# Gating and the front of a recurrent mixer moved into the input projection's stage

## Chip, cores and metric

The kernel runs on one core of a Trainium2 chip. The metric is device time in microseconds (us) of one execution, lower is better. TensorE is called PE here, VectorE DVE, ScalarE ACT, GpSimd Pool, SyncE SP.

## What is computed

A transformer block with a mixture of experts, then two layers (l = 0, 1) of a second block, on 256 tokens of width 1024 in f32. The part of a layer that the change touches:

```python
hn = rms_norm_2(h, g_mix[i])
z = hn @ w_in[i]                                   # 1024 x 2840
z_a, z_b, z_c = split_cols(z, (A_COLS, B_COLS, C_COLS))   # 512, 1024, 1304 columns
y_a = chunked_spatial_gating(z_a, ...)   # gelu, layer_norm of v, causal 128x128 mixing over tokens, times u
# rwkv7_time_mix(z_b, ...): its front
z = z_b + (z_prev - z_b) * mu                      # z_prev: the token before
r, k, v, wd, ad, gd = split_cols(z, B_SIZES)
w_logit = -softplus(-(w0 + tanh(wd) @ w_up)) - 0.5
decay = exp(-exp(w_logit)); a = sigmoid(a0 + ad @ a_up); g = sigmoid(gd) @ g_up
kk = k * k_k, normalised per head;  k = k * (1 + (a - 1) * k_a)
# then a recurrence over the tokens, done by chunks of 64 with cumulated decays
```

## The kernel before, in words

The program is a list of stages. Every engine walks through the list in its own order of instructions; at a stage's end (`end_stage`) all four wait for each other. Only SP, which streams weights from memory into a ring of nine buffers, runs ahead through all stages.

A projection (`stage_project`) takes 512 columns of the weight at a time (the last block of `w_in` is 280 wide), each block in two pieces of four row chunks (128x2048 elements; 128x1120 for the narrow block), so `in_l` has 12 pieces, numbered here 0 to 11. Products are taken in three passes of halves: ACT writes the upper part of a piece (`split_high`, L556), DVE the rest (`split_low`, L560), PE multiplies (L536 to L538), token tile 0 and then tile 1, 12 matmuls each. ACT takes each finished 128x512 result (a job, numbered q, two to a block) out of PSUM into `z` (L2188). In the loop of `evacuate`, iteration i splits the piece `group.size - 1` ahead of piece i, for which piece i - 1 must have been multiplied, and then takes out piece i's jobs where the block is complete. Before the change the group has four upper-part buffers, and the order of blocks is that of z_b and z_c first and z_a last.

After job 5 ACT issues five DMAs (`shift_act`, L2340 to L2344) which copy z_b down by one token into `w_prev`. Pool waits for them and mixes: three operations of 128x1024 for each of two token tiles (L2355 to L2359).

Behind the projection come three stages: `gating(l)`, `rwkv(l)` and `nsa(l)`. The gating has PE transposes (L2236), gelu on ACT (L2245, L2247), a layer norm on DVE, four small matmuls (L2240) and a multiplication on DVE. In `rwkv`, "the front" here is all up to the signal `rw_rkab` (L2614): low-rank inputs on ACT (L2526 to L2528), their transposes (L2369), six matmuls (L2374 to L2376), sigmoids (L2530), decays, cumulated decays by six matmuls and eight tiny ones (L2381, L2385), exponentials (L2538 to L2543), products on DVE (L2609 to L2614). PE's next step, sixteen transposes (L2391), waits for it.

## Time and profile before

| | us |
|---|---|
| median of 3 runs (lowest, highest) | 2702.75 (2701.73, 2703.71) |
| profiled execution, its time | 2700.91 |
| profiled execution, its span | 2699.1 |
| PE, DVE, ACT busy | 2377.1, 1828.3, 1458.9 |

The span runs from the first to the last instruction; the time of an execution holds 1.8 us more. An engine's busy time adds up its instructions over all stages, so it doesn't say which engine sets the pace in one of them.

### The profile page before, as it was taken

Reading aid. Unit: us, or ns where it says so; the run is one execution under the profiler, and the core shown is the slowest. Engines: PE = TensorE matmul, PEld = TensorE weight load, DVE = VectorE, ACT = ScalarE, POOL = GpSimd, SP = SyncE. Lnnn points to the kernel's source line nnn. Section 1 sums busy time; section 2 is a strip of 40 time slices with the busy share of each in tenths; the row PEclk is TensorE's granted clock in tenths of the full one; section 3 lists DMA queues with packets and bytes.
Section 4 is the critical chain, followed back from the end, with each engine's and each line's share of the span. In section 5 each row is a group of like instructions: output and inputs, shape, how many; then the busy total and the mean of one; then the engine's idle time right before and its main releaser. Section 6 shows DMA issues by size and latency. Waiting matters only on the chain. (4 is left out here: it accounts for less than half of the span.)

```text
span 2699.1 us, 30473 instructions
## 1 busy us (share of the span) xinstructions
PE 2377.1 (88%) x12398; PEld 1932.8 (72%) x12398; DVE 1828.3 (68%) x1848; ACT 1458.9 (54%) x1363; POOL 90.9 (3%) x57
## 2 busy tenths in 40 slices
PE   7688478699999999857899986787999999999996
PEld 6566366588888887646678775666888888888884
DVE  5444444688888887446555453557898888898884
ACT  4243122577777775423444443246677767767763
POOL 0200000000000000121000002100000000000000
PEclk9789688899999999868899998898999999999998
DMA  8035024399999998600555444024999998999990
GB/s 260 26 109 171 0 95 139 130 362 366 360 364 361 369 357 322 196 19 11 167 171 187 160 133 134 3 95 161 363 356 358 369 356 294 363 357 358 367 351 31
DMA packets 231968, 617.66 MB, mean 229 GB/s; under 512 B 23164, under 2 KB 68604, under 8 KB 194184
## 3 DMA queue, kind: packets, MB, share of 16 engines
q1 hardware_dynamic: 229728, 609.30, 64.2%
q10 hardware_dynamic: 2088, 6.28, 0.7%
q8 instruction: 102, 1.67, 0.2%
q14 instruction: 50, 0.41, 0.0%
HBM read 612.40 MB, written 1.05 MB: 227 GB/s over the span
## 5 line engine op out<-in xcount | busy, mean ns | idle before, releaser
L560 DVE TENSOR_TENSOR ring_parts<-ring,high_parts 128x2048 fp32r<-128x2048 f32 (+1 forms) x574 | 1287.2, 2284 | 232.4 <-ACT high_parts L556 212.8
L556 ACT CAST high_parts<-ring 128x2048 fp32r<-128x2048 f32 (+1 forms) x574 | 1078.7, 1897 | 258.6 <-PE ps L538 226.3
L538 PE MATMUL ps<-high_parts,arena_parts 128*128 128x512 f32 (+2 forms) x1560 | 618.7, 397 | 0.0
L536 PE MATMUL ps<-high_parts,hT_parts 128*128 128x512 f32 (+2 forms) x1120 | 448.8, 401 | 37.5 <-DVEq L440 22.1
L537 PE MATMUL ps<-ring_parts,hT_parts 128*128 128x512 f32 (+2 forms) x1120 | 443.3, 396 | 0.0
L536 PE MATMUL ps<-high_parts 128*128 128x512 f32 x912 | 365.3, 401 | 0.0
L537 PE MATMUL ps<-ring_parts,high_parts 128*128 128x512 f32 x912 | 359.1, 394 | 0.0
L538 PE MATMUL ps<-high_parts 128*128 128x512 f32 x912 | 356.5, 391 | 0.0
L538 PEld LDWEIGHTS ps<-high_parts,arena_parts 128*128 128x128 f32 x1560 | 298.1, 191 | 68.9
L536 PE MATMUL ps<-high_parts,arena_parts 128*128 128x512 f32 x744 | 294.7, 396 | 11.7 <-ACTq L440 4.5
L537 PE MATMUL ps<-ring_parts,arena_parts 128*128 128x512 f32 x744 | 293.3, 394 | 0.0
L536 PEld LDWEIGHTS ps<-high_parts,hT_parts 128*128 128x128 f32 x1120 | 215.8, 193 | 89.2 <-DVEq L440 25.0
L537 PEld LDWEIGHTS ps<-ring_parts,hT_parts 128*128 128x128 f32 x1120 | 215.7, 193 | 49.6 <-issue 0.2
L538 PEld LDWEIGHTS ps<-high_parts 128*128 128x128 f32 x912 | 171.4, 188 | 41.8
L536 PEld LDWEIGHTS ps<-high_parts 128*128 128x128 f32 x912 | 172.1, 189 | 37.7
L537 PEld LDWEIGHTS ps<-ring_parts,high_parts 128*128 128x128 f32 x912 | 171.0, 187 | 35.8
L536 PEld LDWEIGHTS ps<-high_parts,arena_parts 128*128 128x128 f32 x744 | 140.4, 189 | 45.9 <-ACTq L440 4.9
L537 PEld LDWEIGHTS ps<-ring_parts,arena_parts 128*128 128x128 f32 x744 | 140.6, 189 | 32.3
L2069 DVE SCALAR_TENSOR_TENSOR arena<-ps,arena 128x512 f32<-128x512 f32 x80 | 57.9, 723 | 147.7 <-PE ps L538 132.5
L1985 ACT CAST arena_parts<-ps 128x512 fp32r<-128x512 f32 x80 | 45.4, 567 | 140.3 <-PE ps L1883 140.3
L538 PE MATMUL ps<-high_parts,hT_parts 128*128 128x512 f32 x304 | 120.0, 395 | 0.0
L2003 ACT ACTIVATE arena<-ps 128x512 f32<-128x512 f32 x80 | 46.4, 580 | 68.2 <-PE ps L538 68.2
(523 smaller groups left out, 1932.6 us busy)
## 6 DMA issues: line engine op xcount, KB each, us to landing
ring<-in_moe_w SPq DMA_DIRECT2D x248, 1024.0 KB, 5.4
ring<-in_w_gate SPq DMA_DIRECT2D x64, 1024.0 KB, 5.9
ring<-in_w_up SPq DMA_DIRECT2D x64, 1024.0 KB, 5.7
ring<-in_w_down SPq DMA_DIRECT2D x64, 1024.0 KB, 5.8
ring<-in_w_in SPq DMA_DIRECT2D x46, 1024.0 KB, 5.1
ring<-in_ffn_w SPq DMA_DIRECT2D x44, 512.0 KB, 5.0
ring<-in_moe_w SPq DMA_DIRECT2D x32, 512.0 KB, 5.0
ring<-in_w_out SPq DMA_DIRECT2D x12, 1024.0 KB, 5.3
```

The source lines that it names most:

```text
L536: pe.matmul(dst, a_hi, b_hi, start=first, stop=False, skip_group_check=True)
L537: pe.matmul(dst, a_hi, b_lo, start=False, stop=False, skip_group_check=True)
L538: return pe.matmul(dst, a_lo, b_hi, start=False, stop=last, skip_group_check=True)
L556: act.copy(high_flat(p), raw_flat(p)).then_inc(upper, 1)
L560: dve.tensor_tensor(raw_flat(p, ring_parts_flat), raw_flat(p), f32(high_flat(p)), ALU.subtract).then_inc(split, 1)
L1985: act.copy(m_hidT[:, 0:st.n // P, :].rearrange("p c n -> p (c n)"), ps[:, TURN, 0:st.n])\
L2003: act.activation(m_sg[:, 0:st.n], ps[:, GATE, 0:st.n], ACT.Silu).then_inc(sig("moe_silu"), 1)
L2069: dve.scalar_tensor_tensor(out=m_hid[:, 0:st.n], in0=src, scalar=m_gate[:, q:q + 1], in1=m_sg[:, 0:st.n], op0=ALU.mult, op1=ALU.mult).then ...
```

## The change

`gating(l)` as a stage goes. Its operations and the whole front of `rwkv` become `front(l)`: hooks that the loops of the projection `in_l` call at written-out places. PE's hooks come after a token tile of a piece (slot = 2 x piece + tile): 6, 16, 17, 18 and 19. ACT's and DVE's hooks come in iteration i of `evacuate`, before the jobs are taken out (`after` = 0) or behind (`after` = 1). The blocks' order becomes z_b (pieces 0 to 3), z_a (4, 5), then z_c (6 to 11, the last two narrow). The upper-part buffers of `in_l` are three, not four. The shift DMAs are issued after job 3, not within job 5. Mixing of token tile 0 stays on Pool, tile 1 goes to DVE. Tanh is computed by a sigmoid; a mask `tri_aft` takes the place of `same_chunk`, so that one subtraction (L2607) and one copy (L2537) go. Results of the gating wait in `s_sq`, and Pool copies them to `ycat` at the start of `rwkv`.

```diff
-            blocks = [(c0, min(512, (width if c0 >= first else first) - c0))
-                      for c0 in list(range(first, width, 512)) + list(range(0, first, 512))]
+            starts = list(range(0, width, 512))
+            if first:
+                starts = starts[1:3] + starts[0:1] + starts[3:]
+            blocks = [(c0, min(512, width - c0)) for c0 in starts]
...
-            for groups in (group_in, group_out, group_ple):
-                groups.append(Group(4))
+            for groups, size in ((group_in, 3), (group_out, 4), (group_ple, 4)):
+                groups.append(Group(size))
...
+                    if hook:
+                        hook(pe, 2 * p.at + j.tile)
...
+                    hook(eng, i, 0)
+                for j in p.jobs if p.last else []:
...
-                        if after and j.q == after[0]:
-                            after[1](eng)
...
+                if hook:
+                    hook(eng, i, 1)
...
+                    dve.tensor_tensor(tri_aft[:], tri_aft[:], tri_inc[:], ALU.subtract)
...
-            group_in[l].high = highs(13872, 11824, 9776, 7728)
+            group_in[l].high = highs(13872, 11824, 9776)
...
+        MW.at = 15920
+        w_prev = MW.take(NT, 1024)
+        MW.at = 15920
+        w_R, w_K, w_A, w_Ke = [half_t() for _ in range(4)]
+        w_lw, w_a, w_g, w_kk, w_km, w_B, w_Be, w_lora = [half_t() for _ in range(8)]
...
+        def mix(eng, l, t):
+
+            done = sig("rw_mixing_pool" if t == 0 else "rw_mixing_dve")
+            zb_t = z[:, t, ZB0:ZC0]
+            eng.tensor_tensor(w_prev[:, t, :], w_prev[:, t, :], zb_t, ALU.subtract).then_inc(done, 1)
+            eng.wait_ge(done, 2 * l + 1)
+            eng.tensor_tensor(w_prev[:, t, :], w_prev[:, t, :], l_mu[:], ALU.mult).then_inc(done, 1)
+            eng.wait_ge(done, 2 * l + 2)
+            eng.tensor_tensor(zb_t, zb_t, w_prev[:, t, :], ALU.add).then_inc(sig("rw_mixed"), 1)
...
         def mix_pool(pool, l):
-
             pool.memset(w_prev[0:1, 0, :], 0.0).then_inc(sig("rw_first"), 1)
             pool.wait_ge(sig("rw_first"), l + 1)
-            pool.wait_ge(sig("rw_prev"), 80 * (l + 1))
...
-                pool.tensor_tensor(zb_t, zb_t, w_prev[:, t, :], ALU.add).then_inc(sig("rw_mixed"), 1)
+            mix_wait(pool, l)
+            mix(pool, l, 0)
...
+
+            def pe_(pe, slot):
+                if slot == 6:
+                    pe.wait_ge(sig("layer_params"), 16 * N_LAYER_LOADS * (l + 1))
+                    for h in range(AH):
+                        mm = pe.transpose(ps[:, 4, h * P:(h + 1) * P], l_ws[:, h, :], ident[:])
+                    mm.then_inc(sig("gat_wT"), 1)
+                elif slot == 16:
...
+                    pe.wait_ge(*at("rw_lora"))
+                    for k in range(2):
+                        for t in range(NT):
+                            mm = pe.transpose(ps[:, 4, k * S + t * P:k * S + (t + 1) * P], w_lora[:, t, k * P:(k + 1) * P], ident[:])
+                    mm.then_inc(sig("rw_loT_psum"), 1)
+                elif slot == 17:
+                    pe.wait_ge(*at("rw_loT"))
+                    for t in range(NT):
+                        tok = slice(t * P, (t + 1) * P)
...
+                    mm.then_inc(sig("rw_lin"), 1)
+                elif slot == 18:
+                    pe.wait_ge(sig("gat_v"), l + 1)
+                    for h in range(AH):
+                        mm = pe.matmul(ps[:, 4, h * P:(h + 1) * P], s_wT[:, h, :], s_v[:, :, h, :], start=True, stop=True)
...
+                    pe.wait_ge(*at("rw_lw"))
+                    pe.wait_ge(*at("rw_g"))
+                    for k, m in enumerate((tri_inc, tri_str, tri_aft)):
+                        for t in range(NT):
+                            pe.matmul(ps[:, 5 + k, t * BW:(t + 1) * BW], m[:], w_lw[:, t, :], start=True, stop=True)
+                    pe.wait_ge(sig("gat_out"), l + 1)
+                    for t in range(NT):
...
+                    mm.then_inc(sig("rw_cum"), 1)
+
+            def act_(act, i, after):
+                if (i, after) == (3, 1):
+                    shift_act(act, l)
+                elif (i, after) == (5, 1):
+                    act.wait_ge(evac_act, jobs_of[f"in_{l}"][5].evac)
+                    act.activation(s_v.rearrange("p t h n -> p t (h n)"), z[:, :, AW:2 * AW], ACT.Gelu_apprx_tanh)\
+                        .then_inc(sig("gat_gelu"), 1)
+                    act.activation(s_u, z[:, :, 0:AW], ACT.Gelu_apprx_tanh).then_inc(sig("gat_gelu"), 1)
+                elif (i, after) == (7, 0):
+                    act.wait_ge(sig("gat_var"), l + 1)
+                    act.activation(small[:, 24:32], small[:, 16:24], ACT.Sqrt).then_inc(sig("gat_sd"), 1)
+                    act.wait_ge(*at("rw_kk2"))
+                    act.activation(w_root, w_most, ACT.Sqrt).then_inc(sig("rw_kkrt"), 1)
+                    act.copy(w_lora[:, :, 64:128], z[:, :, ZB0 + 832:ZB0 + 896])
+                    act.activation(w_lora[:, :, 0:64], z[:, :, ZB0 + 768:ZB0 + 832], ACT.Sigmoid, scale=2.0)
+                    act.activation(w_lora[:, :, 128:256], z[:, :, ZB0 + 896:ZB0 + 1024], ACT.Sigmoid).then_inc(sig("rw_lora"), 1)
+                elif (i, after) == (9, 0):
+                    act.wait_ge(*at("rw_logit"))
+                    act.activation(w_lw, w_lw, ACT.Sigmoid).then_inc(sig("rw_sig"), 1)
+                    act.activation(w_a, w_a, ACT.Sigmoid).then_inc(sig("rw_sig"), 1)
+                    act.copy(flat2(w_g), ps[:, 7, :]).then_inc(sig("rw_g"), 1)
+                elif (i, after) == (10, 1):
+                    act.wait_ge(*at("rw_cum"))
+                    act.activation(flat2(w_R), ps[:, 5, :], ACT.Exp)
+                    act.activation(flat2(w_K), ps[:, 5, :], ACT.Exp, scale=-1.0).then_inc(sig("rw_total"), 1)
+                    act.activation(flat2(w_A), ps[:, 6, :], ACT.Exp)
+                    act.activation(w_cend, ps[:, 4, 0:8], ACT.Exp).then_inc(sig("rw_cend"), 1)
+                    act.activation(flat2(w_Ke), ps[:, 7, :], ACT.Exp).then_inc(sig("rw_exp"), 1)
+
...
+                if after:
+                    return
+                if i == 4:
+                    dve.wait_ge(sig("gat_wT"), l + 1)
+                    dve.tensor_tensor(s_wT, ps[:, 4, :].rearrange("p (h n) -> p h n", h=AH),
...
+                elif i == 5:
+                    mix_wait(dve, l)
+                    mix(dve, l, 1)
+                elif i == 6:
+                    dve.wait_ge(sig("gat_gelu"), 2 * l + 1)
+                    vstep(dve, dve.tensor_reduce(small[:, 0:8], v8, AX, ALU.add))
...
+                    dve.tensor_scalar(small[:, 16:24], small[:, 0:8], 1.0 / HD, LN_EPS, ALU.mult, ALU.add).then_inc(sig("gat_var"), 1)
+                elif i == 7:
+                    dve.wait_ge(sig("rw_mixed"), NT * (l + 1))
+                    vstep(dve, dve.tensor_tensor(w_kk, zk, row(2), ALU.mult))
+                    vstep(dve, dve.tensor_tensor(w_B, w_kk, w_kk, ALU.mult))
+                    vstep(dve, dve.tensor_reduce(w_ss, w_B.rearrange("p t (h n) -> p (t h) n", h=BH), AX, ALU.add))
+                    dve.tensor_scalar(w_most, w_ss, 1e-24, None, ALU.max).then_inc(sig("rw_kk2"), 1)
+                    dve.wait_ge(sig("gat_sd"), l + 1)
+                    vstep(dve, dve.reciprocal(small[:, 0:8], small[:, 24:32]))
+                    vstep(dve, dve.tensor_tensor(v8, v8, small[:, 0:8].unsqueeze(2).to_broadcast([P, 8, HD]), ALU.mult))
...
+                elif i == 8:
+                    dve.wait_ge(*at("rw_loT_psum"))
+
+                    dve.tensor_scalar(w_loT[0:64, 0, :], ps[0:64, 4, 0:S], 2.0, -1.0, ALU.mult, ALU.add)
+                    dve.tensor_copy(w_loT[64:128, 0, :], ps[64:128, 4, 0:S])
+                    dve.tensor_copy(w_loT[:, 1, :], ps[:, 4, S:2 * S]).then_inc(sig("rw_loT"), 1)
+                    dve.wait_ge(*at("rw_kkrt"))
+                    vstep(dve, dve.reciprocal(w_ss, w_root))
...
+                elif i == 9:
+                    dve.wait_ge(*at("rw_lin"))
+                    dve.tensor_tensor(w_lw, ps[:, 5, :].rearrange("p (t n) -> p t n", t=NT), row(0), ALU.add)
+                    dve.tensor_tensor(w_a, ps[:, 6, :].rearrange("p (t n) -> p t n", t=NT), row(1), ALU.add)\
+                        .then_inc(sig("rw_logit"), 1)
...
+                    dve.tensor_scalar(flat2(w_lw), flat2(w_lw), -float(np.exp(-0.5)), None, ALU.mult).then_inc(sig("rw_lw"), 1)
+                    dve.wait_ge(sig("gat_mixed"), l + 1)
+                    dve.wait_ge(sig("gat_gelu"), 2 * l + 2)
+                    for h in range(AH):
+                        ins = dve.scalar_tensor_tensor(out=s_sq[:, :, h, :], in0=ps[:, 4, h * P:(h + 1) * P].rearrange("p (t n) -> p t n", t=NT),
+                                                       scalar=l_bsT[:, h:h + 1], in1=s_u[:, :, h * HD:(h + 1) * HD],
+                                                       op0=ALU.add, op1=ALU.mult)
...
+                    dve.wait_ge(*at("rw_sig", 2))
+
+                    vstep(dve, dve.scalar_tensor_tensor(out=w_km, in0=w_a, scalar=-1.0, in1=row(3), op0=ALU.add, op1=ALU.mult))
+                    vstep(dve, dve.scalar_tensor_tensor(out=w_km, in0=w_km, scalar=1.0, in1=zk, op0=ALU.add, op1=ALU.mult))
+                    vstep(dve, dve.tensor_tensor(flat2(w_B), flat2(w_kk), flat2(w_a), ALU.mult))
+                elif i == 11:
+                    dve.wait_ge(*at("rw_total"))
+                    dve.tensor_tensor(w_R, w_R, zr, ALU.mult)
+                    dve.wait_ge(*at("rw_cend"))
+                    dve.scalar_tensor_tensor(out=flat2(w_A), in0=flat2(w_kk), scalar=-1.0, in1=flat2(w_A), op0=ALU.mult, op1=ALU.mult)
+                    dve.wait_ge(*at("rw_exp"))
+                    vstep(dve, dve.tensor_tensor(flat2(w_Be), flat2(w_B), flat2(w_Ke), ALU.mult))
+                    dve.tensor_tensor(flat2(w_Ke), flat2(w_km), flat2(w_Ke), ALU.mult)
+                    vstep(dve, dve.tensor_tensor(flat2(w_B), flat2(w_B), flat2(w_K), ALU.mult))
+                    dve.tensor_tensor(flat2(w_K), flat2(w_K), flat2(w_km), ALU.mult).then_inc(sig("rw_rkab"), 1)
+
+            return pe_, act_, dve_
...
-                with_before(stage_project(f"in_{l}", (hT_parts, low_2), z_copy_act, act_after=(5, lambda act, l=l: shift_act(act, l)), norm=f"mix{l}",
+                with_before(stage_project(f"in_{l}", (hT_parts, low_2), z_copy_act, norm=f"mix{l}", hooks=front(l),
...
-                gating(l),
...
+                pool.tensor_copy(ycat[:, :, 0:AW].rearrange("p t (h n) -> p t h n", h=AH), s_sq)
```

## Rows read from the trace of the kernel before

**Rows 1.** The page's costliest groups: the splits of a weight piece (busy us, mean ns).
```profile
L560 DVE TENSOR_TENSOR ring_parts<-ring,high_parts 128x2048 fp32r<-128x2048 f32 (+1 forms) x574 | 1287.2, 2284 | 232.4 <-ACT high_parts L556 212.8
L556 ACT CAST high_parts<-ring 128x2048 fp32r<-128x2048 f32 (+1 forms) x574 | 1078.7, 1897 | 258.6 <-PE ps L538 226.3
```

**Rows 2.** Windows: layer 0's projection, two stages behind it, layer 1's two stages together.
```profile
core 0: us, PE busy (x) PEld busy (x) DVE busy (x) ACT busy (x) POOL busy (x), PEclk, DMA share, GB/s
1096.50:1161.40 64.90, 64.02 (x288) 52.28 (x288) 25.49 (x13) 28.47 (x28) 19.17 (x7) 0.97 0.59 186
1161.40:1172.60 11.20, 2.73 (x12) 2.20 (x12) 7.19 (x15) 5.21 (x6) 0.00 (x0) 0.57 0.00 0
1172.60:1199.30 26.70, 12.42 (x37) 8.21 (x37) 12.10 (x21) 9.46 (x16) 0.00 (x0) 0.56 0.00 0
...
1651.30:1687.90 36.60, 13.87 (x49) 9.34 (x49) 19.29 (x35) 14.66 (x22) 0.00 (x0) 0.64 0.09 29
```

**Rows 3.** Timeline of PE: what the front held up (start us, length, instructions).
```profile
1199.30 3.67 PE L2391 MATMUL ps<-ident,arena 128*128 128x128 f32 x16 [8.50 <-DVE arena L2614]
```

**Rows 4.** Windows of PE: gating L2236, L2240; front L2374 to L2376, L2381 to L2385.
```profile
1161.40:1162.10 0.70, 0.66 (x4) 1.00 0.00 0
1169.37:1171.50 2.13, 2.07 (x8) 0.50 0.00 0
...
1176.97:1181.66 4.69, 4.68 (x12) 0.50 0.00 0
1184.16:1190.81 6.65, 6.64 (x20) 0.54 0.00 0
```

**Rows 5.** Windows of DVE: gating L2259-L2264, L2266-L2270; front L2585-L2586, L2589-L2590, L2611-L2614.
```profile
1163.38:1166.66 3.28, 3.10 (x6) 0.50 0.00 0
1166.93:1169.32 2.39, 2.28 (x4) 0.50 0.00 0
1172.79:1174.22 1.43, 1.38 (x2) 0.50 0.00 0
1176.83:1177.72 0.89, 0.85 (x3) 0.50 0.00 0
1196.50:1199.25 2.75, 2.67 (x5) 0.50 0.00 0
```

**Rows 6.** Windows of ACT: low-rank inputs L2526 to L2528; exponentials L2538 to L2541.
```profile
1172.67:1174.90 2.23, 2.20 (x4) 0.50 0.00 0
...
1192.72:1194.38 1.66, 1.65 (x4) 0.79 0.00 0
```

**Rows 7.** Timeline of ACT: jobs 1, 3 and 11 taken out, shift DMAs issued.
```profile
1109.62 0.69 ACT L2188 ACTIVATE arena<-ps,rstd 128x512 f32<-128x512 f32 x1 [2.05 <-PE ps L538]
...
1120.83 0.69 ACT L2188 ACTIVATE arena<-ps,rstd 128x512 f32<-128x512 f32 x1 [2.11 <-PE ps L538]
...
1129.23 1.27 ACTq L2340 DMA_DIRECT2D arena<-arena  x2
...
1133.17 0.57 ACTq L2344 DMA_DIRECT2D arena<-arena  x1
...
1160.64 0.69 ACT L2188 ACTIVATE arena<-ps,rstd 128x512 f32<-128x512 f32 x1 [2.11 <-PE ps L538]
```

**Rows 8.** Timeline of POOL: mixing begins.
```profile
1139.32 2.41 POOL L2355 TENSOR_TENSOR arena<-arena 128x1024 f32<-128x1024 f32 x1 [41.79 <-issue]
1141.81 4.35 POOL L2357 TENSOR_TENSOR arena<-arena 128x1024 f32<-128x1024 f32 x1
```

**Rows 9.** Timeline of DVE: the split of a wide piece beside the mixing.
```profile
1139.61 4.27 DVE L560 TENSOR_TENSOR ring_parts<-ring,high_parts 128x2048 fp32r<-128x2048 f32 x1 [2.42 <-ACT high_parts L556]
```

**Rows 10.** Windows of PE: granted clock (PEclk) early in the projection.
```profile
1098.10:1101.70 3.60, 3.60 (x10) 0.53 1.03 369
1101.70:1109.50 7.80, 7.80 (x35) 1.00 0.27 80
```

**Rows 11.** Timeline of SP: the last of layer 0's parameter loads is issued.
```profile
1092.55 0.43 SPq L788 DMA_DIRECT2D arena<-in_nsa_vc_w  x1
```

More of the change, by code:

```diff
@@ L586, in pe_project, with evacuate @@
                         mm.then_inc(proj_done, 1)
-        def evacuate(eng, name, engine, copy=None, after=None, between=None, norm=None):
+                    if hook:
+                        hook(pe, 2 * p.at + j.tile)
+        def evacuate(eng, name, engine, copy=None, between=None, norm=None, hook=None):
             if norm is not None:
@@ L2289, in emit @@
+        assert MG.at <= 9776
         MW = Arena(arena)
```

189 lines of the change are left out of this document (48 added, 141 removed).

## The prediction

> **What bounds the kernel now.** I read the windows by stage first, since the page's busy shares average over stages with different limits. In layer 0's projection PE is busy 64.0 of 64.9 us at a granted clock of 0.97 (2.4 GHz nearly throughout): PE sets the pace there, and DVE (25.5) and ACT (28.5) have room [rows 2]. In the two stretches behind it nobody is busy half the time: the gating takes 11.2 us with PE busy 2.7, the front 26.7 with PE busy 12.4, at clocks of 0.57 and 0.56, which is the 1.2 GHz level most of the time. Together 37.9 us in layer 0 and 36.6 in layer 1 [rows 2]. The timeline of PE shows why: it stands idle until a product on DVE is done, here 8.5 us before the sixteen transposes [rows 3]. It is one chain from engine to engine, which an overlap with the projection could hide. DMA moved nothing there (last column 0), so the ring of weights was full and time saved here isn't lost to a late weight.
>
> **The frame.** At most 37.9 and 36.6 us can go. What stays on the path is the work that PE itself takes over, and what PE must wait for at its five slots. I walk layer 0 through on its own clock.
>
> PE's pace: jobs 1 and 3 are taken out at 1109.6 and 1120.8, so a wide piece takes 5.6 us and a token tile 2.8. Jobs 3 to 11 are 39.8 us apart for six wide and two narrow pieces, so a narrow one takes 3.1 [rows 7]. A piece costs ACT 1.9 and DVE 2.3 us to split [rows 1], a narrow one by its size 1.1 and 1.3.
>
> PE's added work: four transposes took 0.66 at full clock; L2240 took 2.1, the six low-rank matmuls 4.7, the cumulations 6.65, all at half clock [rows 4]. At full clock I take 0.6, 0.6, 1.0, 2.4 and 3.3, 7.9 us together; at half clock all the way it is about 15.
>
> **Slot 6** (after tile 0 of piece 3, 1118): four transposes, 0.6. It waits for the layer's parameters, whose last load was issued at 1092.5 [rows 11], 25 us earlier: no cost. Pieces 3 to 7 then end 0.6 later: 1121.4, 1127.0, 1132.6, 1138.2, 1143.8. Behind PE's wait at a slot stand all later pieces, and through `used` SP's loads; with a full ring SP's lateness costs nothing.
>
> **The shift DMAs.** ACT issues five in 4.5 us (1129.2 to 1133.7), and Pool's mixing starts 5.6 later [rows 7, 8]. They now follow job 3: issue 1122.1 to 1126.5, landed 1132.2. Queued behind them on ACT is the split of piece 6 (to 1128.8); PE wants that piece at 1132.6. DVE's part ends 1131.2: hidden, with 1.4 us to spare, so three buffers in place of four cost nothing here. The gelus (one table load and 1.2) end by 1136.3, and ACT's splits of pieces 8 and 9 at 1138.2 and 1140.5.
>
> **The mixing** decides most. Pool took 2.41 alone and 4.35 when DVE was splitting; that split took 4.27 in place of 2.28 [rows 1, 8, 9]. The added times are 1.94 and 1.99: they take turns, and both finish one operation in the sum of the two. A DVE mixing operation isn't in the trace; at half the elements of a split I take 1.2 (the bounds: 0.7 for 512 columns in [rows 5], 2.4 as on Pool). Pool's first waits for the split of piece 7 (1131.9 to 1134.2), then they alternate: 3 x 2.4 + 3 x 1.2 = 10.8, so 1145.0. If they didn't block each other DVE would be through at 1137.8.
>
> The Trainium skill (Perfetto Trace Analysis, Optimizing Scalar/DVE Operations) warns that work moved between GpSimd and DVE may not help, because they share a read port. By that rule at its strongest the mixing takes 14.5 us, as six operations on Pool would, and the predicted time is 7 us longer.
>
> **What is late next: DVE.** It splits piece 8 only behind the mixing, 1145.0 to 1147.3; PE wants it at 1143.8 and stalls 3.5 us. Then the layer norm's first part, 3.3, to 1150.6; split of piece 9, to 1152.9; kk and its norm, 1.4 + 0.9 [rows 5], to 1155.2. ACT, waiting in iteration 7, then needs the root and the low-rank inputs with one table load, 2.2 for the latter [rows 6], 2.5 in all: 1157.8.
>
> The Trainium skill (ScalarE: Activation LUTs, What ACT_TABLE_LOAD costs) counts 2.66 us for a switch of table sets, drain included. The row has three operations and a load in 2.23 [rows 6], so the trace doesn't show the drain; by the page the time would be 3 us longer over both layers.
>
> **Slot 16** is reached at 1150.1 to 1151 and waits until 1157.8: some 7 us of stall. After a gap the projection's clock was 0.53 for 3.6 us before it returned to 1.00 [rows 10]. So transposes and tile 1 run partly at half clock, to 1162.5 or so. **Slot 17**: ACT takes out jobs 6 and 7 and splits piece 10 (1160.2), DVE splits it (1161.5) and copies three parts out of PSUM, 1.1 us: 1162.6, no further wait. The low-rank matmuls end 1165 to 1167; I take 1166. DVE's additions (1.3), ACT's sigmoid (0.6) and DVE's scaling (0.4) run beside tile 0 of piece 9 (to 1168.8) and the gating's matmuls of **slot 18** (1169.8); DVE's second half of the layer norm (2.4) had ended by 1157.6. Tile 1 ends 1172.6, **slot 19** 1175.9 (decays ready since 1169, the gating's product since 1171.5), the narrow pieces 10 and 11 at 1182.1. Beside them ACT has four exponentials in 1.7 [rows 6] and a fifth of 0.6 (1178.6), DVE its last four products in 2.75 [rows 5]: 1181.4, just under the cover of piece 11. Without this cover it would cost up to 5. Last job and stage end, 0.7 and 0.1 as before [rows 2, 7], with a little for half clock: 1183.4.
>
> **The sum.** The transposes start at 1183.4, not 1199.3: 15.9 us in layer 0. The same 22.0 us behind the old end of the projection in place of 36.6 is 14.6 in layer 1 [rows 2]. The sixteen transposes took 3.67 with PE cold [rows 3]; behind dense pieces they run at the 2.4 GHz level: 1.5 each (bounds 0 and 1.8). Pool's copy to `ycat` lies where Pool waited anyway, 1.2 without that cover. Sum: 15.9 + 14.6 + 3.0 = 33.5. The profiled execution had 2700.9 us (span and 1.8), 1.85 under the median: 2667.4, or 2669 on the median's footing.
>
> **The rivals.**
> *No blocking on Pool's port for this mix.* Slot 16's signal comes 7 us earlier in both layers, and less of the rest runs cold: 2669 - 16 = 2653. For it: only one clear pair of operations is in my rows. Against: the sums fit to 0.05 us. 0.12.
> *Sharing buys nothing* (3.7 us more per layer, the turns costing as much as six operations on Pool): 2676. Against it stands that each side's extra time was just the other's work. 0.05.
> *The clock stays low to slot 18 or 19.* In the front PE ran at 0.50 for a whole 4.7 us of matmuls, and through nearly all of the next 6.65 [rows 4]. Half clock to slot 18 adds 2 + 2.8 + 1 = 6 per layer, to slot 19 about 10: 2681 to 2689. 0.17.
> *No gain.* Half clock from piece 8 to the end of the stage: 48 wide matmuls' worth of pieces (11.2), the narrow ones (6.2) and the small ones of slots 16 to 19 (7) doubled, less what I counted (3) and what stalls cover (5): 16, as much as is won. 2701. Against it: the cold stretch of rows 10 ended under dense matmuls. 0.03.
> *Slower.* The split of piece 6 is late behind ACT's DMA issues (its slack is 1.4 us), PE stalls there already, and the clock stays at half from piece 6 to the end. That is 11 more for pieces 6 and 7: 27 per layer against 16.6 won, 2723. It decides as soon as more than 16.6 us a layer are lost. 0.02.
> Likeliest, as walked: 0.61, with its own range of 2661 to 2677 (4 us a layer for the clock's return and the DVE operations' bounds).
>
> **How the numbers follow.** 2669 is the likeliest case. The range of 2650 to 2687 takes in the case without blocking and most of the low-clock one; outside are the last of that, no gain and slower. About 0.2% (5 us) is what a measurement of this kernel tells from no change: faster 0.95, same 0.03, slower 0.02.
>
> **What the profile would show.** The projections' windows 20 to 24 us longer, no gating stage, PE's wait before L2391 gone. PE's longest wait in the projection at the transposes of the low-rank inputs, on ACT, 5 to 8 us, and a shorter one on DVE's split of piece 8. Pool's and DVE's mixing operations in turns, ending some 12 us after the DMAs landed. A granted clock near half for some us behind the stall. I am wrong if the DVE mixing ends before Pool's second operation, if PE waits longer at slot 17 or 19 than at 16, or if a wait for a weight's split shows up ahead of piece 8.

## The result, and the profile after

The changed kernel takes 2662.17 us (median of four runs, 2661.25 to 2663.54) against 2702.65 (2701.73 to 2703.71) for the kernel before: ratio 0.985, 95% interval 0.9833 to 0.9868, 40.5 us less. Forecast were 2669.0 and a range of 2650 to 2687. The profiled execution took 2663.54 (span 2661.8). One execution of the kernel before, in the first series of experiments, ran in a slow state (5009 us) and is left out of every number here.

I divide the span at the first squares of each norm (ACT) and call "the turn" the start of the sixteen transposes [rows 3]. The windows of the kernel before, both layers, up to the turn and behind it:

```profile
1096.56:1199.30 102.74, 79.17 (x337) 62.69 (x337) 44.78 (x48) 43.12 (x50) 19.17 (x7) 0.82 0.37 117
1199.30:1343.12 143.82, 115.36 (x1454) 92.94 (x1455) 82.69 (x226) 51.68 (x122) 13.42 (x10) 0.82 0.29 84
1588.44:1687.86 99.42, 75.88 (x333) 60.04 (x332) 45.22 (x48) 42.94 (x51) 18.27 (x6) 0.86 0.42 133
1687.86:1821.23 133.37, 105.73 (x1448) 86.68 (x1448) 79.46 (x221) 46.81 (x115) 13.45 (x10) 0.88 0.15 48
```

The same four windows after (columns as in [rows 2]):

```profile
1094.24:1178.35 84.11, 75.97 (x336) 60.98 (x336) 51.64 (x52) 39.44 (x47) 10.09 (x4) 0.92 0.46 143
1178.35:1319.80 141.45, 113.31 (x1454) 91.26 (x1455) 82.38 (x226) 51.83 (x121) 13.54 (x11) 0.83 0.27 85
1565.18:1648.07 82.89, 73.90 (x333) 59.34 (x331) 51.77 (x52) 39.44 (x48) 9.93 (x3) 0.93 0.46 138
1648.07:1779.16 131.09, 103.82 (x1448) 84.27 (x1448) 79.80 (x221) 46.70 (x116) 13.54 (x11) 0.90 0.18 58
```

Up to the turn 18.6 us are gone in layer 0 and 16.5 in layer 1, behind it 2.4 and 2.3. That is 39.8 us over both mixers. In the other stages, which the change doesn't touch, the profiled execution lost 2.5 us net: the stretch ahead of layer 0's norm is 2.3 shorter, the one behind layer 1's mixer 4.8 longer. Layer 0's norm starts 2.3 us earlier than before: add 2.3 to a time of layer 0 below to set it beside the prediction's clock.

Timeline of PE after, the instructions that waited (layer 0, layer 1):

```profile
1144.25 0.80 PE L538 MATMUL ps<-high_parts,hT_parts 128*128 128x512 f32 x1 [2.92 <-DVE ring_parts L562]
1154.32 1.08 PE L2344 MATMUL ps<-ident,arena 128*128 128x128 f32 x4 [4.58 <-ACT arena L2387]
1178.35 1.97 PE L2484 MATMUL ps<-ident,arena 128*128 128x128 f32 x16 [0.62 <-ACTq L442]
...
1612.92 0.50 PE L538 MATMUL ps<-high_parts,hT_parts 128*128 128x512 f32 x1 [2.55 <-DVE ring_parts L562]
1622.98 1.09 PE L2344 MATMUL ps<-ident,arena 128*128 128x128 f32 x4 [5.82 <-ACT arena L2387]
1648.07 1.97 PE L2484 MATMUL ps<-ident,arena 128*128 128x128 f32 x16 [0.62 <-ACTq L442]
```

Two waits are left: at piece 8 for DVE's split, at slot 16 for ACT's low-rank inputs. The 8.50 us ahead of the transposes [rows 3] are 0.62, and the transposes take 1.97 for 3.67. Slots 17, 18 and 19 waited for nothing.

Timeline of Pool after, the mixing of tile 0:

```profile
1131.60 2.59 POOL L2310 TENSOR_TENSOR arena<-arena 128x1024 f32<-128x1024 f32 x1 [36.39 <-issue]
1134.27 3.29 POOL L2312 TENSOR_TENSOR arena<-arena 128x1024 f32<-128x1024 f32 x1
1137.63 3.27 POOL L2314 TENSOR_TENSOR arena<-arena 128x1024 f32<-128x1024 f32 x1
```

Timeline of DVE after, tile 1, the late split of piece 8, and the last sum of squares:

```profile
1131.82 3.46 DVE L2310 TENSOR_TENSOR arena<-arena 128x1024 f32<-128x1024 f32 x1
1135.31 3.33 DVE L2312 TENSOR_TENSOR arena<-arena 128x1024 f32<-128x1024 f32 x1
1138.67 3.32 DVE L2314 TENSOR_TENSOR arena<-arena 128x1024 f32<-128x1024 f32 x1
1141.92 2.28 DVE L562 TENSOR_TENSOR ring_parts<-ring,high_parts 128x2048 fp32r<-128x2048 f32 x1
...
1151.65 0.17 DVE L2427 TENSOR_SCALAR small<-small 128x8 f32<-128x8 f32 x1
```

Timeline of ACT after, the chain to slot 16's signal:

```profile
1147.41 0.21 ACT L2382 ACTIVATE small<-small 128x8 f32<-128x8 f32 x1 [8.38 <-DVE small L2421]
1151.86 0.21 ACT L2384 ACTIVATE small<-small 128x8 f32<-128x8 f32 x1 [4.24 <-DVE small L2427]
1151.97 0.28 ACT L2385 COPY arena<-arena 128x128 f32<-128x128 f32 x1
1152.26 1.28 ACT L2386 ACT_TABLE_LOAD   x1
...
1153.77 0.40 ACT L2387 ACTIVATE arena<-arena 128x256 f32<-128x256 f32 x1
```

Read together: mixing to 1142.0, split of piece 8 to 1144.2, where PE's wait ends; then DVE's layer norm, a split and the sums of squares, ACT's second root at 1151.86, its low-rank inputs at 1154.2, where PE's other wait ends. The inputs themselves need only the mixing.

PE's clock around the two waits and from there to the turn, in windows of PE after:

```profile
1144.20:1149.80 5.60, 5.49 (x12) 0.50 0.28 108
1154.30:1157.20 2.90, 2.88 (x9) 0.53 0.00 0
1157.20:1178.30 21.10, 20.53 (x120) 1.00 0.16 50
```

Tile 0 of piece 8 ran at the 1.2 GHz level (5.5 us for 2.8), 2.9 us behind slot 16 likewise, the rest at 2.4 GHz.

### The profile page after: what moved, and what is told of

It is laid out like the page before. It is cut to its first block and busy times, and to the rows that moved or that the text cites. A ratio compares the mean times of both kernels' runs of the same rounds, so it can differ in the third digit from the quotient of the medians.

```text
span 2661.8 us, 30466 instructions
## 1 busy us (share of the span) xinstructions
PE 2373.4 (89%) x12398; PEld 1929.3 (72%) x12398; DVE 1842.2 (69%) x1857; ACT 1451.5 (55%) x1357; POOL 73.7 (3%) x53
## 5 line engine op out<-in xcount | busy, mean ns | idle before, releaser
L562 DVE TENSOR_TENSOR ring_parts<-ring,high_parts 128x2048 fp32r<-128x2048 f32 x574 | 1284.6, 2280 | 228.2 <-ACT high_parts L558 206.8
L558 ACT CAST high_parts<-ring 128x2048 fp32r<-128x2048 f32 x574 | 1078.5, 1897 | 269.1 <-PE ps L540 231.4
```

The lines of the kernel that those rows point to most:

```text
L558: act.copy(high_flat(p), raw_flat(p)).then_inc(upper, 1)
L562: dve.tensor_tensor(raw_flat(p, ring_parts_flat), raw_flat(p), f32(high_flat(p)), ALU.subtract).then_inc(split, 1)
```

## Experiments

The table has all twelve runs. "To the turn" is from the first squares of the norm to the transposes, layer 0 / layer 1, in the profiled execution. The first four, the next four and the last four each shared a chip with runs of the kernel before, whose medians were 2701.30, 2703.73 and 2700.89. In the last series the kernel before ranged from 2689.65 to 2714.40, so a few us between two medians are not a difference.

| kernel | median (lowest to highest) | ratio to before, 95% | to the turn |
|---|---|---|---|
| mix_all_dve | 2651.57 (2651.12 to 2653.54) | 0.9817, 0.98 to 0.9835 | 80.3 / 79.7 |
| mix_all_pool | 2661.47 (2656.64 to 2668.64) | 0.986, 0.9833 to 0.9887 | 84.1 / 83.5 |
| front_back | 2683.62 (2678.72 to 2686.18) | 0.9937, 0.9919 to 0.9954 | 94.2 / 90.2 |
| gating_back | 2681.36 (2680.25 to 2681.88) | 0.9925, 0.9907 to 0.9942 | 91.6 / 89.5 |
| lora_first | 2662.88 (2661.64 to 2670.58) | 0.9858, 0.9819 to 0.9897 | 85.2 / 83.1 |
| combined | 2651.01 (2646.95 to 2655.62) | 0.9811, 0.9771 to 0.985 | 77.8 / 75.3 |
| combined_shared | 2654.13 (2652.74 to 2657.56) | 0.9825, 0.9787 to 0.9864 | 80.0 / 77.6 |
| late_shift | 2680.16 (2673.77 to 2683.25) | 0.9915, 0.9887 to 0.9943 | 93.8 / 92.7 |
| changed_again | 2659.31 (2656.75 to 2666.46) | 0.9853, 0.9816 to 0.9889 | 84.6 / 82.0 |
| all_dve_again | 2654.91 (2648.94 to 2660.01) | 0.9831, 0.9796 to 0.9866 | 82.6 / 78.8 |
| combined_again | 2652.68 (2645.03 to 2655.53) | 0.9812, 0.9776 to 0.9848 | 77.3 / 74.7 |
| warm_wait | 2662.84 (2653.74 to 2666.91) | 0.985, 0.9813 to 0.9887 | 85.8 / 82.5 |

### Which part earned the time: front_back and gating_back

Each undoes one half of the move. front_back leaves the gating in the projection and puts the front back into `rwkv`, with the low-rank inputs ahead of the root there as before (the added lines stand in `rwkv`, ahead of the sixteen transposes):

```diff
-                elif slot == 16:
-                    pe.wait_ge(sig("gat_wm"), l + 1)
-                    pe.wait_ge(*at("rw_lora"))
...
-                elif slot == 17:
-                    pe.wait_ge(*at("rw_loT"))
...
-                elif slot == 19:
-                    pe.wait_ge(*at("rw_lw"))
...
...
+                pe.wait_ge(*at("rw_lora"))
...
+                pe.wait_ge(*at("rw_loT"))
...
+                pe.wait_ge(*at("rw_lw"))
```

> The front of the recurrent mixer (all from the low-rank inputs and kk to the products) goes back to the start of its own stage; gating and mixing stay in the projection. By the walk of the prediction: of 11.2 us of gating per layer some 1.6 us stay as PE's own work and 2.9 to 3.5 as the stall ahead of piece 8, and the front is 2 us shorter than it was (one subtraction and one copy gone): 8 to 9 us per layer under the kernel before, about 2686. If what was gained came mostly from the front's new place this kernel lies nearer 2703 than 2662; if gating carried it, nearer 2662.

gating_back leaves the front in the projection and puts the gating back as a stage of its own:

```diff
-                elif slot == 18:
-                    pe.wait_ge(sig("gat_v"), l + 1)
-                    for h in range(AH):
-                        mm = pe.matmul(ps[:, 4, h * P:(h + 1) * P], s_wT[:, h, :], s_v[:, :, h, :], start=True, stop=True)
-                    mm.then_inc(sig("gat_mixed"), 1)
...
+        def gating(l):
```

> Gating alone goes back to a stage of its own behind the projection; front and mixing stay in the projection. DVE then has 5.5 us less ahead of the low-rank parts, so the signal for the low-rank transposes comes 3 us earlier, and PE's four small matmuls go from the projection: the projection ends 4 to 4.5 us earlier than in the changed kernel, and 11.2 us of gating come back: 6.5 to 7 us per layer slower than the changed kernel, about 2675.5. If PE's wait was set by ACT or by the clock and not by DVE's queue, the projection keeps its length less 1.6, and the time is about 2681.

Timeline of PE, front_back, layer 0:

```profile
1172.80 2.05 PE L2416 MATMUL ps<-arena,tri_inc 128*128 128x256 f32 x4 [3.19 <-ACT arena L2570]
...
1184.47 3.68 PE L2426 MATMUL ps<-ident,arena 128*128 128x128 f32 x16 [5.23 <-DVE arena L2647]
```

Timeline of PE, gating_back, layer 0:

```profile
1148.17 0.66 PE L2340 MATMUL ps<-ident,arena 128*128 128x128 f32 x4 [1.31 <-ACT arena L2370]
...
1179.52 2.05 PE L2442 MATMUL ps<-arena 128*128 128x128 f32 x8 [7.45 <-DVE arena L2473]
1182.83 3.68 PE L2494 MATMUL ps<-ident,arena 128*128 128x128 f32 x16 [1.26 <-DVEq L442]
```

Window of gating_back, layer 1, from the turn to the next norm (all engines):

```profile
1658.89:1796.57 137.68, 110.87 (x1448) 90.01 (x1448) 79.68 (x221) 45.43 (x114) 13.54 (x11) 0.84 0.14 46
```

Against the median of the changed kernel, taken in another series, front_back is 21.4 us slower and gating_back 19.2: together 40.6, about the whole gain. How exactly the halves add up the medians can't tell. In the profiles the turn comes 10.1 and 7.4 us later without the front, 7.5 and 6.6 without the gating, 31.5 together, and in both kernels the transposes are cold in both layers (3.68 for 1.97), 1.7 us more each time. So both halves earned a good part of the gain.

front_back came within 3 us of its 2686. gating_back was expected at 2675.5 and took 2681.4. To the turn it is as expected, 6.5 to 7 us a layer. The miss lies behind the turn: the cold transposes, 1.7 us a layer, which I had left out, and in layer 1 some 5 us more, since the stretch took 137.7 us in place of 131.1 at a granted clock of 0.84 in place of 0.90. Such a difference between profiles comes up again below, and its cause is open. The gating also held DVE from the low-rank work: without it slot 16 waited 1.31 us in place of 4.58 (3.74 in place of 5.82 in layer 1), and slot 17 waited 1.28.

### Sharing the mixing: mix_all_dve and mix_all_pool

The first gives both token tiles to DVE, the second to Pool; the edit of the first (the other is its mirror image):

```diff
-            done = sig("rw_mixing_pool" if t == 0 else "rw_mixing_dve")
+            done = sig("rw_mixing_dve")
...
-            pool.wait_ge(sig("rw_first"), l + 1)
-            mix_wait(pool, l)
-            mix(pool, l, 0)
...
+                    dve.wait_ge(sig("rw_first"), l + 1)
                     mix_wait(dve, l)
+                    mix(dve, l, 0)
                     mix(dve, l, 1)
```

> All six mixing operations go to DVE (tile 0 and tile 1), Pool keeps only its memset. Theory A (Pool and DVE take turns on a shared port, so sharing costs DVE the time of Pool's operations): on DVE alone six operations of 1.1 us take 6.7 us in place of the 10.2 that the three shared pairs took, so the mixing ends 3.5 us earlier, PE's 2.9 us stall ahead of piece 8 goes, the wait at the low-rank transposes stays near 6 us but ends 3.3 us earlier: about 6.5 us faster than the changed kernel, 2655.5. Theory B (sharing halves the work, the turns are not what holds DVE): twice the operations on DVE make the mixing as late or later, 2662 to 2669.

> All six mixing operations on Pool, as in the kernel before, at the new place. Theory A: Pool needs 14.1 us plus the DVE operations that it takes turns with, and ends at about 20 us after the DMAs landed; DVE's split of piece 8 is no longer late (the 2.9 us stall goes) but kk and the low-rank inputs come some 2 us later, PE waits 12 us there: 3 to 6 us slower than the changed kernel, about 2667. Theory B (the place of the mixing doesn't matter, PE's wait is ACT's or the clock's): within 1 us of 2662.

Timeline of DVE, mix_all_dve, layer 0 (first and last of six operations, then the split of piece 8):

```profile
1128.06 1.22 DVE L2310 TENSOR_TENSOR arena<-arena 128x1024 f32<-128x1024 f32 x1
...
1134.23 1.22 DVE L2314 TENSOR_TENSOR arena<-arena 128x1024 f32<-128x1024 f32 x1
1135.37 2.28 DVE L562 TENSOR_TENSOR ring_parts<-ring,high_parts 128x2048 fp32r<-128x2048 f32 x1
```

Timeline of PE, mix_all_dve, layer 0, its only long wait up to the turn:

```profile
1147.77 1.08 PE L2341 MATMUL ps<-ident,arena 128*128 128x128 f32 x4 [7.00 <-ACT arena L2384]
```

Timeline of Pool, mix_all_pool, layer 0, two of the six operations:

```profile
1129.00 2.42 POOL L2312 TENSOR_TENSOR arena<-arena 128x1024 f32<-128x1024 f32 x1
...
1138.25 2.68 POOL L2312 TENSOR_TENSOR arena<-arena 128x1024 f32<-128x1024 f32 x1
```

Timeline of DVE, mix_all_pool, layer 0, beside Pool's mixing:

```profile
1133.49 0.67 DVE L2414 TENSOR_REDUCE small<-arena 128x8 f32<-128x512 f32 x1
1134.19 1.66 DVE L2415 TENSOR_SCALAR small<-small 128x8 f32<-128x8 f32 x1
1135.88 2.83 DVE L2416 TENSOR_TENSOR arena<-arena,small 128x512 f32<-128x512 f32 x1
```

A mixing operation takes 1.22 us on DVE alone and 2.42 on Pool alone; a pair in turns takes 3.3. So the three pairs took 10.4 us where DVE alone does all six in 7.4 (1128.06 to 1135.45). Sharing makes the mixing 3 us longer, and DVE's later work moves by as much. In layer 1, where the mixing starts within 0.3 us of the same place in both kernels, the turn comes 3.2 us later with sharing. In layer 0 it comes 3.8 later, but there the shift DMAs were already issued 1.6 us later, which is no effect of sharing; in the pair that ran side by side the difference in layer 0 is 2.0. With all six on DVE the stall ahead of piece 8 goes, slot 16 waits 7.00 us, and the kernel is faster than the changed one: 10.6 us by the medians of two series, 4.4 where both ran side by side (all_dve_again, below). With all six on Pool the mixing takes 17.4 us and ends 5 us later than shared in layer 0, at 52.8 us after the norm's start (6.4 later in layer 1). But DVE does the layer norm and splits beside it, slower, and its sums of squares end as early as in the changed kernel (57.3 against 57.6; layer 1: 56.4 against 55.3). PE has no stall ahead of piece 8 and waits 11.47 us at slot 16. The turn comes as early in layer 0, where the DMAs were issued 1.6 us earlier, and 0.6 us later in layer 1: next to no difference, where I had expected some 5 us more.

The Trainium skill (SBUF — State Buffer, SBUF: two separate sides) says that GpSimd and DVE's second port pair are one exclusive lock, held for a whole instruction, and that a DVE operation with two inputs in the on-chip memory needs it against a GpSimd operation that reads there. This trace agrees in the main: the operations with two inputs took turns with Pool's, though a pair took 3.3 us and not the full 1.22 + 2.42 = 3.64, while the reduction, with one input, took its ordinary 0.67 us (0.69 elsewhere in that timeline) amid Pool's. The small operation behind it, of 128x8, took 1.66 us in place of 0.17.

### The wait at slot 16: lora_first, combined, combined_shared

lora_first lets ACT compute the low-rank inputs ahead of both roots:

```diff
                 elif (i, after) == (7, 0):
+                    act.wait_ge(sig("rw_mixed"), NT * (l + 1))
+                    act.copy(w_lora[:, :, 64:128], z[:, :, ZB0 + 832:ZB0 + 896])
+                    act.activation(w_lora[:, :, 0:64], z[:, :, ZB0 + 768:ZB0 + 832], ACT.Sigmoid, scale=2.0)
+                    act.activation(w_lora[:, :, 128:256], z[:, :, ZB0 + 896:ZB0 + 1024], ACT.Sigmoid).then_inc(sig("rw_lora"), 1)
                     act.wait_ge(sig("gat_var"), l + 1)
...
-                    act.copy(w_lora[:, :, 64:128], z[:, :, ZB0 + 832:ZB0 + 896])
```

> The mixing stays shared between Pool and VectorE. ScalarE computes the three activations of the low-rank inputs (128x256) ahead of the two square roots, as soon as the mixing is done, instead of behind them. In the changed kernel these activations end at 1154.17, 12.2 us after the mixing, because the second root waits for VectorE's sums of squares (1151.8), and TensorE waits 4.58 us (layer 0) and 5.82 us (layer 1) at slot 16 for them. Theory A (that wait is on the path that sets the end): the signal comes about 5 to 6 us earlier, slot 16 no longer waits; slot 17's matmuls then wait for VectorE's copies of the low-rank transposes, which stand behind its sums of squares (end 1151.8 at the earliest), so that about 2 to 3 us of the wait stay. The turn becomes 2 us shorter in each layer; 2658 us. Theory B (the path to the end runs through the narrow pieces' splits or the normalization on VectorE, and slot 16 only gives a place to wait): the wait moves behind slot 18 and nothing is gained, 2661 to 2664 us. Theory C (three more activations ahead of the root delay the normalization of the keys by two table loads): 1 to 2 us slower a layer, 2665 us.

Timeline of PE, lora_first, layer 0:

```profile
1146.87 0.50 PE L538 MATMUL ps<-high_parts,hT_parts 128*128 128x512 f32 x1 [3.08 <-DVE ring_parts L562]
...
1149.77 0.60 PE L2344 MATMUL ps<-ident,arena 128*128 128x128 f32 x4
...
1159.47 0.79 PE L2350 MATMUL ps<-arena 64*128 64x256 f32 x1 [6.30 <-DVE arena L2439]
```

The wait at slot 16 is gone and stands at slot 17, 6.30 us (layer 1: 4.91), for DVE's copies, which are behind the sums of squares, the layer norm's second part and the split of piece 10 in its queue. Nothing was gained: the copies came late by as much as the inputs had. Theory A had left a rest of 2 to 3 us, with the copies right behind the sums of squares.

combined therefore also moves DVE's copies to the start of iteration 7 and has all mixing on DVE; combined_shared is the same with the mixing shared:

```diff
                 elif i == 7:
+                    dve.wait_ge(*at("rw_loT_psum"))
+                    dve.tensor_scalar(w_loT[0:64, 0, :], ps[0:64, 4, 0:S], 2.0, -1.0, ALU.mult, ALU.add)
+                    dve.tensor_copy(w_loT[64:128, 0, :], ps[64:128, 4, 0:S])
+                    dve.tensor_copy(w_loT[:, 1, :], ps[:, 4, S:2 * S]).then_inc(sig("rw_loT"), 1)
...
                 elif i == 8:
-                    dve.wait_ge(*at("rw_loT_psum"))
```

> Three edits together: VectorE does all six operations of the mixing (as in mix_all_dve), ScalarE computes the low-rank inputs ahead of the two roots, and VectorE copies the low-rank transposes out of PSUM ahead of its last split of the projection and the sums of squares, instead of behind them. In mix_all_dve the mixing ended 43.4 us after the start of the norm and the low-rank signal came at 55.6, with 7.0 us of TensorE waiting for it at slot 16. Theory A (slot 16's wait is on the path that sets the end, and TensorE's own work is next behind it): the signal comes at about 46 to 47 us, the wait goes, the turn is 5 to 6 us shorter in each layer than in mix_all_dve (about 74.5 us from the norm's start to the transposes, instead of 80): 2641 us, range 2638 to 2646. Theory B (something else, the splits of the narrow pieces or the normalization of the keys, is close behind slot 16's wait): 1 to 3 us a layer are left, 2645 to 2650 us. Theory C (no gain over mix_all_dve): 2651 us.

> The kernel combined, but with the mixing shared between Pool and VectorE as in the changed kernel: it tells what sharing costs where nothing waits for the roots behind the mixing. In the changed kernel against mix_all_dve sharing cost 3.8 and 3.2 us of the turn in layers 0 and 1. Theory A (Pool and VectorE take turns at a tile in the on-chip memory, so that a pair of 128x1024 operations takes 3.3 us where two on VectorE take 2.45): sharing costs 2.5 to 4 us a layer again, 5 to 8 us in all, 2646 to 2650 us. Theory B (sharing cost in the changed kernel only through the stall ahead of piece 8, 2.92 us in layer 0): the same stall comes here, and the cost in layer 1, without that stall, is below 1 us. Theory C (TensorE is the limit once the low-rank inputs are early, so that sharing is hidden): within 2 us of combined.

Timeline of PE, combined, layer 1, its waits from the norm to the turn:

```profile
1611.74 0.48 PE L2347 MATMUL ps<-arena 64*128 64x256 f32 x1 [0.28 <-DVE arena L2427]
...
1622.90 1.20 PE L2361 MATMUL ps<-arena,tri_inc 128*128 128x256 f32 x4 [2.08 <-ACT arena L2390]
1623.90 1.91 PE L2361 MATMUL ps<-arena,tri_str 128*128 128x256 f32 x4
...
1635.13 1.97 PE L2484 MATMUL ps<-ident,arena 128*128 128x128 f32 x16 [0.62 <-ACTq L442]
```

Slot 16 waits no more, slot 17 for 0.28 us. Slot 19 now waits 2.08 us for ACT's sigmoids, and of the cumulations behind that wait those with `tri_str` take 1.91 where they took 1.03. Still the turn comes 2.4 and 4.4 us sooner than in mix_all_dve. Sharing costs 2.1 and 2.3 us of it; the 3.1 us between the medians (2651.0 and 2654.1) are within their spread. But the time of combined, 2651.0, is that of mix_all_dve, 2651.6, from another series: the 2641 of Theory A didn't come.

The edit of DVE's copies alone is what separates combined_shared from lora_first, and the two ran on one chip: the turn comes 5.2 and 5.5 us sooner, and the kernel is 8.8 us faster (2654.13 against 2662.88, ranges apart). Here the front's gain reaches the end.

### Side by side: changed_again, all_dve_again, combined_again

These three are unedited copies of the changed kernel, mix_all_dve and combined, five rounds each on one chip.

> The changed kernel once more, unedited, beside the three that follow, so that differences of 2 to 10 us are read on one chip. Its two norms of the mixers to the final transposes took 84.1 and 82.9 us; these should come again within 1 us if the front's walk is set by instructions and transfers, and the layers' rest (141.5 and 131.1 us) may move with the granted clock by several us. 2659 to 2666 us.

> mix_all_dve once more, beside the changed kernel. Theory A (sharing the mixing costs 3 to 4 us of each layer's front, since the two engines take turns and the last split ahead of piece 8 stands behind VectorE's share): 6 to 11 us faster than changed_again. Theory B (the 10.6 us between the two medians came from the granted clock of that chip's runs): less than 3 us faster.

> combined once more. Its fronts were 2.5 and 4.4 us shorter than those of mix_all_dve, and its median only 0.6 us lower on another chip; the stretch behind the front was as long or 5 us longer at a lower clock. Theory A (the front's gain counts): 3 to 7 us faster than all_dve_again. Theory B (what TensorE saves in waiting it gives back in granted clock behind the front): within 2 us of all_dve_again.

Against changed_again all_dve_again is 4.4 us faster, which lies between its two theories, and combined_again 6.6; between the latter two are 2.2, which this series can't tell from nothing. So of the front's gain of combined over mix_all_dve (2.4 and 4.4 us; 5 and 4 in the profiles of this series) little or nothing is seen in the time. The windows from the turn to the next norm show where some of it stays. Of combined, layer 1 (all engines):

```profile
1635.13:1770.99 135.86, 109.11 (x1448) 88.80 (x1448) 79.67 (x221) 46.69 (x116) 13.52 (x11) 0.85 0.17 56
```

Of all_dve_again, layer 1, to the turn and behind it:

```profile
1558.23:1637.03 78.80, 71.53 (x332) 58.01 (x330) 48.97 (x55) 39.44 (x48) 0.01 (x1) 0.94 0.49 145
1637.03:1768.90 131.87, 103.97 (x1448) 85.11 (x1448) 79.63 (x221) 46.81 (x115) 13.54 (x11) 0.90 0.18 58
```

The same 1448 matmuls take 109.1 us of PE in place of 104.0, at a granted clock of 0.85 in place of 0.90, and the stretch is 4 us longer. It was 135.0 to 135.9 in four profiles with the low-rank inputs first (lora_first, the two of combined, combined_shared) and 129.6 to 131.9 in six of the others (both of the changed kernel, both of mix_all_dve, late_shift, warm_wait); mix_all_pool had 133.1. The kernels whose transposes are cold had 133.4 (before), 134.1 (front_back) and 137.7 (gating_back), 1.7 of it for the transposes. gating_back thus belongs with the long ones though its low-rank inputs come behind the root, and lora_first lost the 4 us without a shorter front: neither that order nor the idle time that PE saved explains the pattern. Layer 0's stretch differs by 2 to 3 us between two profiles of the same kernel (141.5 and 139.6 for the changed kernel, 138.5 and 141.5 for combined). And these are single executions: that of all_dve_again was the fastest of its six, 6 us under its median. What puts the clock into the one pattern or the other I haven't found.

### Two probes: late_shift and warm_wait

late_shift issues the shift DMAs in iteration 5 in place of 3:

```diff
-                if (i, after) == (3, 1):
+                if (i, after) == (5, 1):
                     shift_act(act, l)
```

> The changed kernel, with ScalarE issuing the three transfers that shift the rows of z (into the zeroed tile) behind its evacuation of the sixth piece instead of the fourth, about 11 us later. Theory A (the landing of these transfers sets the start of the mixing, and the mixing sets all that follows): the mixing starts some 9 to 11 us later than 37.5 us after the norm's start, TensorE waits about that much more at slot 16 or ahead of piece 8, and the turn is 8 to 11 us longer in each layer: 2678 to 2684 us. Theory B (Pool's and VectorE's other work sets the start of the mixing, transfers land long before): less than 2 us a layer, 2662 to 2666 us.

Timeline of PE, late_shift, layer 0:

```profile
1151.94 0.79 PE L538 MATMUL ps<-high_parts,hT_parts 128*128 128x512 f32 x1 [12.33 <-DVE ring_parts L562]
1162.00 1.09 PE L2344 MATMUL ps<-ident,arena 128*128 128x128 f32 x4 [5.48 <-ACT arena L2386]
```

The expectation speaks of three transfers; it is the five of the shift. Their issue moved by 10.5 us in either layer, the turn by 9.7 and 9.8, the median by 18.0 (against that of another series). The mixing is on the path with next to no slack, and DVE's split of piece 8 behind it carries its lateness to PE: 12.33 us for 2.92.

warm_wait adds work for PE alone, at slot 16 ahead of the wait:

```diff
                 elif slot == 16:
+                    for k in range(20):
+                        pe.transpose(ps[:, 7, (k % 4) * P:(k % 4 + 1) * P], l_ws[:, k % AH, :], ident[:])
```

> The changed kernel, in which TensorE does 20 extra transposes of 128x128, into a PSUM bank that nothing reads then, at slot 16 ahead of its wait for the low-rank inputs (4.58 and 5.82 us). They fill a wait with work, so that the granted clock stays or comes back to full sooner; nothing else changes. Theory A (the idle time of TensorE in the front costs through its clock too): the half-clock matmuls behind the wait (low-rank matmuls and narrow pieces up to the turn) become 1 to 1.5 us shorter a layer: 2 to 3 us faster than changed_again. Theory B (the extra transposes outlast the wait or take the clock budget away from the stretch behind): the same time or 1 to 3 us slower.

Timeline of PE, warm_wait, layer 0 (the last line is a wide matmul at 1.2 GHz):

```profile
1147.33 2.35 PE L2342 MATMUL ps<-ident,arena 128*128 128x128 f32 x20
1154.40 1.12 PE L2346 MATMUL ps<-ident,arena 128*128 128x128 f32 x4 [4.73 <-ACT arena L2389]
...
1158.30 0.63 PE L539 MATMUL ps<-ring_parts,hT_parts 128*128 128x512 f32 x1
```

No gain. In this profile tile 0 of piece 8 ran at full clock, so the extra transposes only took the time that half clock had taken in the changed kernel; 4.73 us of wait stayed and PE came out of it cold. What a wait filled to its end would be worth is not answered by this run. What it does show: half clock ahead of slot 16 costs next to nothing, since it only eats into the wait there (the wait ends 60.3 us after the norm's start in this profile and 60.1 in that of the changed kernel).

## Why the prediction was right, and its size 7 us off

**What bounds.** Right. The two stretches were a chain with cover to be had under the projection. Of the gating's 11.2 us a layer most went (gating_back: 7.5 and 6.6 us to the turn and 1.7 a layer for cold transposes; the 19.2 between the medians hold some 5 more that are no part of it), of the front's some 26 us a layer less than half (front_back: 10.1 and 7.4 to the turn, and the same 1.7): it keeps PE's own work and the two waits.

**Slot 6 and piece 6.** Right at no cost: no wait for parameters or for the splits of pieces 3 to 7 in the list of PE's waits, so three buffers were enough. ACT split pieces 6 and 7 in one go from 1124.87 on, directly behind the DMA issues.

**The mixing.** Right, with its mechanism. On the prediction's clock it ran from 1133.9 to 1144.3, 10.4 us for 10.8; DVE's operation was taken at 1.2 and measured alone at 1.22, Pool's at 2.4 and 2.42. The pair takes 3.3, not 3.6. The rows had shown that gap already: 4.35 and 4.27 us for a sum of 2.41 + 2.28 = 4.69 [rows 1, 8, 9]. The prediction compared the two added times with each other (1.94 and 1.99) and not with the other engine's operation, so "the sums fit to 0.05 us" is a misreading, though the turns it argues for are real.

**The stall ahead of piece 8.** 2.92 and 2.55 for 3.5. What I didn't foresee is that tile 0 of piece 8 then runs at half clock. It cost nothing, as slot 16 was waiting anyway.

**Slot 16.** Right place, right releaser, second root and all: the signal came at 1156.5 on the prediction's clock for 1157.8. The wait was 4.58 and 5.82 for some 7 (the profile's forecast was 5 to 8), because the signal came 1.3 us earlier and PE arrived a good microsecond later, from the cold tile. ACT's copy, table load and two sigmoids took 2.2 us, the 1.28 of the load in them. The 2.66 us for a switch that the Trainium skill gives (ScalarE: Activation LUTs, What ACT_TABLE_LOAD costs) would again not fit here, and lora_first, with one switch more in each layer, has its turn only 1.1 us later in layer 0 and 0.2 in layer 1.

**Behind slot 16.** This is the term that was mis-sized: 25.6 us from signal to turn were forecast, 24.2 measured. I let the low-rank matmuls end at 1166; they had no wait and the full clock and ended 1163.8. The cumulations took 3.4 as taken (3.3), the narrow pieces 6.3 (6.2), and the exponentials and products stayed under piece 11.

**The sum.** Forecast 15.9 + 14.6 + 3.0 = 33.5. Measured 18.6 + 16.5 + 3.4 (two times 3.67 - 1.97) = 38.5: 5.0 of the 6.8 us by which 2669 was high. In layer 0 that excess of 2.7 is 1.3 from the earlier signal and 1.4 behind it; in layer 1, whose term I took over from layer 0's walk, it is 1.9. The rest is no part of the change: another 1.3 came in the mixers behind the transposes, 2.5 were lost in other stages, and the two profiled executions lie 1.7 below and 1.4 above their medians, 3.1 together.

**The rivals.** *No blocking* is refuted by the two timelines of the mixing and by mix_all_dve. *Sharing buys nothing* came true in its name but not in its price: all on Pool was no slower than shared, since DVE's other work goes in between Pool's operations (mix_all_pool). *The clock stays low* is refuted for the front: 1.00 from 1157.2 on in layer 0. *No gain* and *slower* didn't come near. The warning of the Trainium skill that I cited (Perfetto Trace Analysis, Optimizing Scalar/DVE Operations), that sharing between GpSimd and DVE may not help, holds here, and more than holds: all_dve_again beats changed_again by 4.4 us. I had used it only to ask whether the shared mixing could be 3.7 us longer, and never asked whether DVE alone, at 6 x 1.2 = 7.2 by my own numbers, would beat the 10.8 I had worked out.

## What to carry to other kernels

Work between two dense stages can go under the first even if every step of it depends on the one before, when the chain has room for its length there: of the 74.5 us of the two stages in both layers 38.5 were gained. What stays is PE's own work and the part that holds up the dense stage's helpers, here DVE's split behind the mixing and the low-rank inputs of slot 16. Before sharing elementwise work between Pool and DVE, compare the sum of a pair (here 3.3 us) with two on DVE (2.45). When a wait is taken off a slot, look at the next queue first: lora_first gained nothing until DVE's copies moved as well, which alone was worth 8.8 us (combined_shared against lora_first).

## What the runs showed of the hardware

- A pair of 128x1024 operations, one on Pool and one on DVE, takes 3.3 us, 0.35 less than 1.22 + 2.42; DVE's operation of 128x8 took 1.66 us for 0.17 in the same company, and a reduction wasn't held at all (0.67).
- A stretch of unchanged instructions can run at different granted clocks. The 1448 matmul records behind the turn of layer 1 took 102.4 to 104.0 us in the changed kernel and all_dve_again, and 109.1 and 108.7 in the two profiles of combined, with the same instructions. In those profiles the stretch was 3 to 6 us longer, about as much as the 4.4 us that combined had gained in that layer's front. Whether an edit well ahead of the stretch sets this is not shown. Untouched stages moved as well between the profiles of before and after: 2.3 us less ahead of layer 0's norm, 4.8 more behind layer 1's mixer.
- The length of a wait doesn't tell whether the clock drops behind it: it was at half behind the 2.92 us ahead of piece 8 (changed kernel, layer 0, first matmul 0.80 us), while behind 3.08 us at the same place in lora_first, layer 0, it was full for the whole token tile (0.39 us each). Behind the 2.55 us ahead of piece 8 in layer 1 of the changed kernel it stayed full for six matmuls and fell to half 1.5 us later, under matmuls without a gap (0.61 and 0.63 from 1614.43 on); behind 2.08 us at slot 19 (combined, layer 1) it was 1.00 for 0.6 us and 0.50 from 1624.10 on.
